# The triangular inverse of a gated delta rule: block transposes moved to VectorE, two last levels as small tiles

## Chip, cores and metric

The kernel runs on one core of one Trainium2 chip. The metric is the device time of one execution in microseconds. An execution covers the whole network below, with all weights read from HBM.

## What is computed

Two layers of a hybrid decoder on 256 positions of width 1024, all in float32. Each layer is a half-step SwiGLU FFN (width 2816), a mixer, and a second FFN. The mixer reads one normalised input through one projection whose columns feed three groups of heads: dilated-window attention (4 heads of 64), multi-scale pooling (256 channels), and a gated delta rule (4 heads of 128, chunks of 64 in the reference). The change is in the delta rule's inverse of a lower triangular matrix:

```python
def chunk_gated_delta_rule(q, k, v, g, beta):
    ...
    A = jnp.where(strict, jnp.einsum('nbhid,nbhjd->nbhij', kb, kc) * decay, 0.0)
    eye = jnp.eye(C, dtype=jnp.float32)
    T = lax.linalg.triangular_solve(eye + A, jnp.broadcast_to(eye, A.shape),
                                    left_side=True, lower=True)
    u = T @ vb
    w = T @ (kb * jnp.exp(g)[..., None])
    ...
```

```python
proj = h @ w_in[l]
aq, ak, av, pu, dq, dk, dv, dz, db, da = jnp.split(proj, split_at, axis=-1)
```

## The kernel before, in words

The program is written out by hand for each engine: TensorE, VectorE, ScalarE, GpSimd (POOL) and the DMA queue of SyncE (SP) each run their own list in order, and counting semaphores (`signal`, with `.at(layer, n)`) order them against each other.

**Weights.** Every weight piece of 128 x 1024 (512 KB) lands in one of six slots of `raw`. ScalarE rounds it to a high part `Wh` (`hi`, L1219), VectorE subtracts that to get a low part `Wl` (`lo`, L1647), and a product is then three matmuls, high by high, high by low and low by high (`three`, L660 to L662). The mixer has 33 pieces per layer. `MIX_SLOTS` says which slot each takes; `mix_free` (L1197) says which product must be over before a slot is cast again; `hi_mix(layer, i)` and `lo_mix(layer, i)` are the casts of piece i at the places where they stand in the two lists. The order of the pieces is: eight for attention and pooling, one with the gates, eight for query and key of the delta rule, four for its value, four for its gate z, eight of the output projection.

**Start of the mixer.** `enter_mixer` (L774) runs eight attention half tiles (`att_part`, L760: two pieces for one half of the positions, 24 matmuls of 128x256) and then the gates. `copy_half` (L1422, its copy in L1430) takes each out of PSUM. Parts 6 and 7 are the pooling channels; they are read only behind the inverse. Then come the query/key pieces with a convolution each (first tap on ScalarE, three taps on VectorE, L1834), the value pieces, gates, normalisation, decays, and the products of keys (L946) from which VectorE makes the matrices `LT` and `aT`.

**The inverse.** Here a chunk has 128 positions, so there are eight units (four heads, two halves c of the positions) of 128 x 128. `DT` and `Dm` hold the inverse found so far, one the transpose of the other. It starts from 2x2 blocks (`DT`, L1951), and each level n of `LEVELS = (2, 4, 8, 16, 32, 64)` doubles the block:

- `level_p` (L991): LT by Dm into banks 4 and 5; VectorE masks it into `PM` (L1959);
- `turn_d` (L998, all levels but the first): TensorE transposes `Dm` into banks 6 and 7, and ScalarE copies the new blocks into `DT` (L1527);
- `level_d` (L1015): DT by the even block columns of PM; ScalarE copies the result into `Dm` (L1538), in the last level into `DT` (L1017, L1540).

`Dm` itself comes from eight transposes on TensorE (L959), copied by ScalarE (L1507). V and K are transposed for later use (L966, L970). The casts of pieces 28, 29 and 30 stand behind the first three levels. POOL applies the rotary positions (L624 to L631); their result is transposed within the last level (`turn_qk`, L979). The first product with the finished inverse is L1101. Then follow the state, the scores (L1040, L1042), the pooling (L1132, L1134, L1156), the attention values (L1066 to L1068), and the eight output pieces (`out_product`).

```python
                for n in range(len(LEVELS)):
                    for c in range(HALVES):
                        level_p(n, c)
                    if n:
                        for c in range(HALVES):
                            turn_d(n - 1, c)
                    if n == len(LEVELS) - 1:
                        turn_qk()
                    for c in range(HALVES):
                        level_d(n, c)
```

Of the kernel before, what the change touches and what calls it, by code (L numbers as in the profile page):

```python
# [21 lines left out]
ALU = mybir.AluOpType  # L22
# [82 lines left out]
LEVELS = (2, 4, 8, 16, 32, 64)  # L105
# [10 lines left out]
C_ATT = C_LEVEL + P * len(LEVELS)  # L116
# [10 lines left out]
def constants():  # L127
# [7 lines left out]
    for n, s in enumerate(LEVELS):  # L135
        below = ((r // s) % 2 == 1) & (k // s == r // s - 1)
        c[:, C_LEVEL + n * P:C_LEVEL + (n + 1) * P] = np.where(r == k, 1.0, np.where(below, -1.0, 0.0))
# [30 lines left out]
def build(nc, x, positions, ffn1_norm, ffn1_w_gate, ffn1_w_up, ffn1_w_down, mix_norm, w_in, pool_w,  # L168
# [3 lines left out]
    with ctx:  # L172
# [190 lines left out]
        d0_turned = signal("d0_turned", 2)  # L363
        d_done = signal("d_done", 2 * len(LEVELS))
        p_done = signal("p_done", 2 * len(LEVELS))
        pm_done = signal("pm_done", 2 * len(LEVELS))
        dd_done = signal("dd_done", 2 * len(LEVELS))
        d_turned = signal("d_turned", 2 * len(LEVELS) - 2)
        dt_done = signal("dt_done", 2 * len(LEVELS))
        v_turned = signal("v_turned", 2)  # L370
# [65 lines left out]
        def _(sp):  # L436
# [16 lines left out]
            def load_ffn(layer, f):  # L453
                if f == 1:

                    gate, up, down = FFN[f]
                    for t in range(2):
                        srcs = (cols(gate, layer, t * P), cols(up, layer, t * P), down[layer, t * P:(t + 1) * P, :])
                        for j in range(3):
                            s = 3 * t + j  # L460
                            last = max(i for i in range(MIX_PIECES) if MIX_SLOTS[i] == s)
                            sp.wait_ge(*lo_cast.at(layer, MIX_BASE + last + 1))
                            sp.dma_start(raw[:, s, :] if j == 2 else piece(raw, s), srcs[j]).then_inc(landed[s].sem, 16)
                else:
                    load_tile(layer, f, 0, 0)
                    load_tile(layer, f, 1, 1)
# [6 lines left out]
            for layer in range(DEPTH):  # L473
# [3 lines left out]
                for i in range(MIX_PIECES):  # L477
# [3 lines left out]
                    if i < FIRST_OUT:  # L481
# [3 lines left out]
                                 else COL_DZ + (i - POS_Z) * P)  # L485
# [154 lines left out]
        def _(pe):  # L640
# [119 lines left out]
            def att_part(layer, j, ks, ready=None):  # L760

                g, c = divmod(j, 2)
                s0, s1, t = MIX_SLOTS[2 * g], MIX_SLOTS[2 * g + 1], slice(c * P, (c + 1) * P)
                pair = slice(s0, s1 + 1, s1 - s0)
                b = bank[ATT_BANKS[j]][:, 0:2 * P].rearrange("p (s c) -> p s c", s=2)
                for i in ks:
# [3 lines left out]
                    m = three(b, X0h[:, k, t], X0l[:, k, t], Wh[:, pair, k * P:(k + 1) * P],  # L770
# [3 lines left out]
            def enter_mixer(layer):  # L774
# [17 lines left out]
                for j in range(2, 8):  # L792
                    split(j // 2 * 2 + 1)
                    if j > 2:
                        pe.wait_ge(*att_read.at(layer, (1, 2, 3, 4, 6)[j - 3]))
# [69 lines left out]
            def mixer(layer):  # L865
# [7 lines left out]
                for i in range(8):  # L873
                    split(POS_QK + i)
                    if i == 0:
                        pe.wait_ge(*att_read.at(layer, 8))
# [78 lines left out]
                for c in range(HALVES):  # L955
                    pe.wait_ge(*dt0_done.at(layer, c + 1))
                    pe.wait_ge(*z_act.at(layer, c + 1))
                    for h in range(DN_HEADS):
                        m = nc.tensor.transpose(bank[4 + c][:, h * P:(h + 1) * P], DT[:, 4 * c + h, :], ident)  # L959
                    m.then_inc(d0_turned.sem, 1)  # L960

                for c in range(HALVES):
# [19 lines left out]

                def level_p(n, c):


                    pe.wait_ge(*d_done.at(layer, 2 * n + c + 1))
                    if n == 0:
                        pe.wait_ge(*lt_done.at(layer, c + 1))
                    for h in range(DN_HEADS):
# [5 lines left out]
                def turn_d(n, c):  # L995

                    for h in range(DN_HEADS):
                        m = nc.tensor.transpose(bank[6 + c][:, h * P:(h + 1) * P], Dm[:, 4 * c + h, :], ident)  # L998
                    m.then_inc(d_turned.sem, 1)

                def level_d(n, c):

                    s = LEVELS[n]
# [3 lines left out]
                    else:  # L1007
                        pe.wait_ge(*dt_done.at(layer, 2 * n + c - 1))
                    for h in range(DN_HEADS):
                        u = 4 * c + h  # L1010
                        out = bank[6 + c][:, h * 64:(h + 1) * 64].rearrange("p (n s) -> p n s", s=s)
                        pm = PM[:, u, :].rearrange("p (n a s) -> p n a s", a=2, s=s)
                        dt = DT[:, u, :].rearrange("p (n a s) -> p n a s", a=2, s=s)
                        if n < len(LEVELS) - 1:
                            m = nc.tensor.matmul(out, DT[:, u, :], pm[:, :, 0, :], start=True, stop=True)  # L1015
                        else:
                            m = nc.tensor.matmul(out, PM[:, u, :], dt[:, :, 1, :], start=True, stop=True)  # L1017
                    m.then_inc(dd_done.sem, 1)


                for n in range(len(LEVELS)):
                    for c in range(HALVES):
                        level_p(n, c)
                    if n:
                        for c in range(HALVES):
                            turn_d(n - 1, c)
# [1111 lines left out]
```

## Time and profile before

| what | value |
|---|---|
| median of 3 runs | 1093.78 us (1093.41 to 1094.16) |
| the profiled execution's own time | 1093.62 us |
| its span in the profile | 1091.8 us |
| TensorE (PE) busy | 1060.0 us, 97% of the span |
| VectorE (DVE) busy | 736.9 us, 67% |
| ScalarE (ACT) busy | 616.0 us, 56% |
| GpSimd (POOL) busy | 231.7 us, 21% |
| granted TensorE clock, mean | 0.997 of full speed |
| HBM | 163 GB/s over the span |

The profile is of one execution; its own time is 0.16 us under the median, and 1.8 us of it lie outside the span. Engines are named PE, DVE, ACT, POOL in its rows; PEld is TensorE's loading of weights, which overlaps its matmuls. A matmul of float32 operands shows as two starts in the rows of the trace; a transpose, or a matmul of rounded high and low operands (fp32r), shows as one. Durations of single matmuls overlap, so that the distance from start to start is what one costs. Layer 0's mixer starts near 197 us and ends near 357, layer 1's lies 537.5 us behind it.

### The profile page before, as it was taken

Reading aid. Unit: us, or ns where it says so; the run is one execution under the profiler, and the core shown is the slowest. Engines: PE = TensorE matmul, PEld = TensorE weight load, DVE = VectorE, ACT = ScalarE, POOL = GpSimd, SP = SyncE. Lnnn points to the kernel's source line nnn. Section 1 sums busy time; section 2 is a strip of 40 time slices with the busy share of each in tenths; the row PEclk is TensorE's granted clock in tenths of the full one; section 3 lists DMA queues with packets and bytes.
Section 4 is the critical chain, followed back from the end, with each engine's and each line's share of the span. In section 5 each row is a group of like instructions: output and inputs, shape, how many; then the busy total and the mean of one; then the engine's idle time right before and its main releaser. Section 6 shows DMA issues by size and latency. Waiting matters only on the chain.

```text
span 1091.8 us, 18536 instructions
## 1 busy us (share of the span) xinstructions
PE 1060.0 (97%) x6251; PEld 922.2 (84%) x6251; DVE 736.9 (67%) x1153; ACT 616.0 (56%) x1077; POOL 231.7 (21%) x257
## 2 busy tenths in 40 slices
PE   7999999899999999999999999999999999999997
PEld 6888888798987788888878888888988878888885
DVE  5666666878745766666676666668785657666665
ACT  6555555847644655555665555566665546555554
POOL 2212111295300121121122121112003003211212
PEclk9999999999999999999999999999999999999998
DMA  9766666562312476666646666666532035766660
GB/s 296 238 194 190 191 183 181 139 194 78 135 40 72 141 216 188 192 191 190 183 133 208 194 191 190 183 185 167 162 115 79 2 116 163 207 189 193 190 193 38
DMA packets 251895, 178.23 MB, mean 163 GB/s; under 512 B 5875, under 2 KB 237576, under 8 KB 251720
## 3 DMA queue, kind: packets, MB, share of 16 engines
q1 hardware_dynamic: 250880, 175.66, 54.3%
q0 software_dynamic: 336, 1.71, 0.4%
q8 instruction: 30, 0.49, 0.2%
q10 hardware_dynamic: 632, 0.23, 0.1%
q14 instruction: 17, 0.14, 0.0%
HBM read 176.53 MB, written 1.05 MB: 163 GB/s over the span
## 4 chain that ended last, share of the span: by engine, by line
PE 83%; DVE 10%; ACT 5%; issue 1%; DMA 0%; ACTq 0%; DVEq 0%
PE bank L678 28%; PE bank L681 15%; PE bank L660 11%; PE bank L661 10%; PE bank L662 10%; DVE Wl L1647 4%; PE bank L1015 2%; ACT Wh L1219 1%; DVE X L1692 1%; PE bank L991 1%; DVE xr L1823 1%; PE bank L723 1%; ACT X L1277 1%; DVE VT L1834 1%; DVE early L1865 1%
## 5 line engine op out<-in xcount | busy, mean ns | idle before, releaser
L1647 DVE TENSOR_TENSOR Wl<-raw,Wh 128x1024 fp32r<-128x1024 f32 x330 | 424.6, 1296 | 102.3 <-ACT Wh L1219 102.2
L1219 ACT ACTIVATE Wh<-raw 128x1024 fp32r<-128x1024 f32 x330 | 337.1, 1053 | 78.2 <-PE bank L662 75.6
L678 PE MATMUL bank<-X,Wh 128*128 128x512 f32 x1344 | 334.7, 391 | 0.0
L678 PEld LDWEIGHTS bank<-X,Wh 128*128 128x128 f32 x1344 | 246.7, 188 | 47.6
L577 POOL TENSOR_TENSOR gact<-gact,pooled 128x256 f32<-128x256 f32 x88 | 79.2, 900 | 626.4 <-DVE gact L1743 462.2
L681 PEld LDWEIGHTS bank<-X,Wl 128*128 128x128 f32 x1344 | 183.0, 190 | 14.0 <-DVE Wl L1647 1.2
L681 PE MATMUL bank<-X,Wl 128*128 128x256 f32 x1344 | 187.8, 283 | 0.0
L660 PE MATMUL bank<-Wh,aH 128*128 128x512 f32 x352 | 139.0, 395 | 2.0 <-DVE aL L1764 1.6
L661 PE MATMUL bank<-Wl,aH 128*128 128x512 f32 x352 | 138.0, 392 | 0.0
L662 PE MATMUL bank<-Wh,aL 128*128 128x512 f32 x352 | 137.1, 389 | 0.0
L1316 ACT ACTIVATE dec<-bank 128x256 f32<-128x256 f32 x88 | 33.6, 382 | 123.2 <-PE bank L681 122.2
L1333 ACT ACTIVATE aH<-hid 128x256 fp32r<-128x256 f32 x88 | 36.8, 418 | 92.4 <-DVE hid L1758 92.2
L579 POOL TENSOR_TENSOR gact<-gact,pooled 128x256 f32<-128x256 f32 x88 | 66.9, 760 | 79.9 <-ACT gact L1321 79.9
L660 PE MATMUL bank<-X,Wh 128*128 128x256 f32 x272 | 79.8, 293 | 0.0
L660 PEld LDWEIGHTS bank<-Wh,aH 128*128 128x128 f32 x352 | 66.4, 189 | 15.6 <-issue 4.2
L662 PEld LDWEIGHTS bank<-Wh,aL 128*128 128x128 f32 x352 | 66.1, 188 | 14.5
L1743 DVE TENSOR_TENSOR gact<-bank,dec 128x256 f32<-128x256 f32 x88 | 37.3, 424 | 58.9 <-ACT dec L1316 58.5
L662 PE MATMUL bank<-X,Wl 128*128 128x256 f32 x272 | 76.9, 283 | 0.0
L661 PE MATMUL bank<-X,Wh 128*128 128x256 f32 x272 | 76.8, 283 | 0.0
L661 PEld LDWEIGHTS bank<-Wl,aH 128*128 128x128 f32 x352 | 66.4, 189 | 10.4
L1751 DVE TENSOR_TENSOR hid<-bank,dec 128x256 f32<-128x256 f32 x88 | 37.3, 424 | 49.3 <-ACT dec L1327 49.3
L660 PE MATMUL bank<-Wh,X 128*128 128x256 f32 (+1 forms) x192 | 63.2, 329 | 4.8 <-DVE Wl L1647 3.0
(244 smaller groups left out, 1302.0 us busy)
## 6 DMA issues: line engine op xcount, KB each, us to landing
raw<-in_ffn_w_gate SPq DMA_DIRECT2D x88, 512.0 KB, 4.0
raw<-in_ffn_w_up SPq DMA_DIRECT2D x88, 512.0 KB, 3.7
raw<-in_ffn_w_down SPq DMA_DIRECT2D x88, 512.0 KB, 4.4
raw<-in_w_in SPq DMA_DIRECT2D x50, 512.0 KB, 3.9
raw<-in_w_out SPq DMA_DIRECT2D x16, 512.0 KB, 4.0
cst<-in_consts POOLq DMA_DIRECT2D x1, 1536.0 KB, 7.0
xr<-in_x SPq DMA_DIRECT2D x2, 512.0 KB, 4.4
norm_w<-in_final_norm SPq DMA_DIRECT2D x1, 512.0 KB, 5.7
```

What stands on the lines that cost most here:

```text
L577: nc.gpsimd.tensor_tensor(gact[:, par, :], gact[:, par, :], rB, ALU.mult).then_inc(gate_scaled.sem, 1)
L579: nc.gpsimd.tensor_tensor(gact[:, par, :], gact[:, par, :], rB, ALU.mult).then_inc(silu_scaled.sem, 1)
L660: nc.tensor.matmul(outp, lh, rh, start=start, stop=False)
L661: nc.tensor.matmul(outp, lh, rl, start=False, stop=False)
L662: return nc.tensor.matmul(outp, ll, rh, start=False, stop=stop)
L678: nc.tensor.matmul(b[:, :], piece(Wh, s)[:, k, :], X[:, k, :, :], start=k == 0, stop=False)
L681: m = nc.tensor.matmul(b[:, SEQ:], piece(Wl, s)[:, k, :], Xh[:, k, :], start=False, stop=k == KT - 1)
L1219: return nc.scalar.activation(Wh[:, s, :], raw[:, s, :], ACT.Copy).then_inc(hi_cast.sem, 1)
L1333: nc.scalar.activation(aH[:, par, :], hid[:, par, :], ACT.Copy).then_inc(ah_done.sem, 1)
L1647: return nc.vector.tensor_tensor(Wl[:, s, :], raw[:, s, :], Wh[:, s, :].bitcast(F32), ALU.subtract).then_inc(lo_cast.sem, 1)
L1743: nc.vector.tensor_tensor(gact[:, par, :], gbank[par][:, 0:SEQ], low[:, 0, par, :], ALU.add).then_inc(gsum_done.sem, 1)
L1751: nc.vector.tensor_tensor(hid[:, par, :], ubank[par][:, 0:SEQ], low[:, 1, par, :], ALU.add).then_inc(usum_done.sem, 1)
```

## The change

Six things change together.

1. *Attention half tiles.* Parts 6 and 7 (the pooling channels) leave `enter_mixer`. `att_late` runs them within the inverse, from the normalised input `Xh`, `Xl` instead of `X0h`, `X0l`, into banks 2 and 3, so that their copy needs no scale. Their two weight pieces move from positions 6 and 7 to 23 and 24 (`POS_LATE`), all pieces between come two positions earlier, and `MIX_SLOTS`, `mix_free` and the order in which the second FFN's first weights are loaded (slots 3, 4, 0, 1, 5, 2 instead of 0 to 5) follow.
2. *Transposes.* `turn_d` and the eight first transposes on TensorE go, and ScalarE's copies of their results with them. VectorE transposes all 32x32 blocks of four units in one instruction, `Dm` from `DT` once and `DT` from `Dm` once a level (`turn_blocks`). That is enough while no block is larger than 32.
3. *Even block columns.* `level_p` computes, and VectorE masks, only the 64 of 128 columns that `level_d` reads. The masks in the constants are half as wide. There are four levels left, 2 to 16.
4. *The level 32* works on blocks of 32x32 (`quarter_p`, `quarter_d`): 16 and 24 matmuls of 32 rows and 32 columns. The mask is a multiplication by -1 on 32 columns, and ScalarE copies three 32-row blocks for each half, two of them straight into `DT`.
5. *The level 64* works on blocks of 64x64 (`half_p`, `half_d`): 8 matmuls each, into the upper right block of `DT`.
6. *Casts.* Piece 28 keeps its place behind the first level. Pieces 29 and 30 are cast on ScalarE behind the inverse, on VectorE behind the output norms, `out_norm(1)`.

```diff
-POS_GATES, POS_QK, POS_V, POS_Z, FIRST_OUT = 8, 9, 17, 21, 25
-ATT_BANKS = (0, 1, 2, 0, 1, 2, 0, 2)
-MIX_SLOTS = [0, 1, 3, 4, 2, 5] * 4 + [0, 2, 5, 1, 3, 4, 0, 2, 5]
+POS_GATES, POS_QK, POS_V, POS_Z, POS_LATE, FIRST_OUT = 6, 7, 15, 19, 23, 25
+ATT_EARLY = 6
+ATT_BANKS = (0, 1, 2, 0, 1, 2, 2, 3)
+MIX_SLOTS = [0, 1, 3, 4, 2, 5] * 3 + [0, 1, 3, 4, 2, 0, 1] + [5, 3, 4, 2, 0, 1, 5, 2]
...
-LEVELS = (2, 4, 8, 16, 32, 64)
+LEVELS = (2, 4, 8, 16)
+N_LEVELS = len(LEVELS) + 2
+EVEN = P // 2
...
+                def att_late(j):
+
+                    split(POS_LATE + 1)
+                    pe.wait_ge(*z_act.at(layer, j - ATT_EARLY + 3))
+                    att_part(layer, j, range(KT)).then_inc(att_in.sem, 1)
...
-                    for h in range(DN_HEADS):
-                        u = 4 * c + h
-                        m = nc.tensor.matmul(bank[4 + c][:, h * P:(h + 1) * P], LT[:, u, :], Dm[:, u, :],
-                                             start=True, stop=True)
+                        pe.wait_ge(*d0_done.at(layer, c + 1))
+                        pe.wait_ge(*z_act.at(layer, c + 1))
+                    else:
+                        pe.wait_ge(*d_done.at(layer, 2 * (n - 1) + c + 1))
+                    for h, u in units(c):
+                        even = Dm[:, u, :].rearrange("p (n a s) -> p n a s", a=2, s=LEVELS[n])[:, :, 0, :]
+                        m = nc.tensor.matmul(bank[4 + c][:, h * EVEN:(h + 1) * EVEN], LT[:, u, :], even, start=True, stop=True)
...
+                def quarter_p(c):
+
+                    pe.wait_ge(*d_done.at(layer, 6 + c + 1))
+                    for h, u in units(c):
+                        for i in range(2):
+                            even, odd = slice(64 * i, 64 * i + 32), slice(64 * i + 32, 64 * i + 64)
+                            m = nc.tensor.matmul(bank[4 + c][odd, h * 32:(h + 1) * 32], LT[even, u, odd], Dm[even, u, even],
+                                                 start=True, stop=True)
+                    m.then_inc(p_done.sem, 1)
+
+                def quarter_d(c):
+
+
+                    pe.wait_ge(*pm_done.at(layer, 8 + c + 1))
+                    pe.wait_ge(*dt_done.at(layer, 6 + c + 1))
+                    q = [slice(32 * i, 32 * i + 32) for i in range(4)]
+                    for h, u in units(c):
+                        at = slice(h * 32, (h + 1) * 32)
+                        nc.tensor.matmul(bank[6 + c][q[1], at], DT[q[1], u, q[1]], PM[q[1], u, 0:32], start=True, stop=True)
+                        nc.tensor.matmul(bank[6 + c][q[0], at], PM[q[1], u, 0:32], DT[q[1], u, q[1]], start=True, stop=True)
+                        m = nc.tensor.matmul(bank[6 + c][q[2], at], PM[q[3], u, 0:32], DT[q[3], u, q[3]],
+                                             start=True, stop=True)
+                    m.then_inc(dd_done.sem, 1)
...
                 for n in range(len(LEVELS)):
                     for c in range(HALVES):
                         level_p(n, c)
-                    if n:
-                        for c in range(HALVES):
-                            turn_d(n - 1, c)
-                    if n == len(LEVELS) - 1:
-                        turn_qk()
                     for c in range(HALVES):
                         level_d(n, c)
+                for c in range(HALVES):
+                    quarter_p(c)
+                att_late(6)
+                for c in range(HALVES):
+                    quarter_d(c)
+                turn_qk()
+                for c in range(HALVES):
+                    half_p(c)
+                att_late(7)
+                for c in range(HALVES):
+                    half_d(c)
...
+                    dve.wait_ge(*dt0_done.at(layer, c + 1))
+                    nc.vector.transpose(Dm[:, u, :].rearrange("p u d -> p (u d)"),
+                                        DT[:, u, :].rearrange("p u d -> p (u d)")).then_inc(d0_done.sem, 1)
                 for i in (25, 26, 27):
                     lo_mix(layer, i)
```

**The order of the instructions, TensorE, from the transposes of V (VT) and K (QK) to the end of the second level.** In the rows `four` is the arena that holds LT, Dm and DT, and `x8` is eight in a row. Before:

```order
L959 MATMUL bank<-cst,four 128x128 x8
L966 MATMUL bank<-cst,VT 128x128 x8
L970 MATMUL bank<-cst,QK 128x128 x4
L991 MATMUL bank<-four 128x128 x8
L1015 MATMUL bank<-PM,four 128x64 x8
L991 MATMUL bank<-four 128x128 x8
L998 MATMUL bank<-cst,four 128x128 x8
L1015 MATMUL bank<-PM,four 128x64 x8
```

Now:

```order
L965 MATMUL bank<-cst,VT 128x128 x8
L969 MATMUL bank<-cst,QK 128x128 x4
L1001 MATMUL bank<-four 128x64 x8
L1012 MATMUL bank<-PM,four 128x64 x8
L1001 MATMUL bank<-four 128x64 x8
L1012 MATMUL bank<-PM,four 128x64 x8
```

The transposes with the identity (`cst`) are gone, and the first product of a level has 64 columns instead of 128.

**VectorE, from the matrix of 2x2 blocks (four<-four,cst) to the second of the levels.** Before:

```order
L1951 TENSOR_TENSOR four<-four,cst 128x512 x2
L1647 TENSOR_TENSOR Wl<-raw,Wh 128x1024 x3
L1959 TENSOR_TENSOR PM<-bank,cst 128x512 x2
L1647 TENSOR_TENSOR Wl<-raw,Wh 128x1024
L1959 TENSOR_TENSOR PM<-bank,cst 128x512 x2
L1647 TENSOR_TENSOR Wl<-raw,Wh 128x1024
```

Now:

```order
L1999 TENSOR_TENSOR four<-four,cst 128x512
L2001 STREAM_TRANSPOSE four<-four 128x512
L1999 TENSOR_TENSOR four<-four,cst 128x512
L2001 STREAM_TRANSPOSE four<-four 128x512
L1694 TENSOR_TENSOR Wl<-raw,Wh 128x1024 x3
L2018 TENSOR_TENSOR PM<-bank,cst 128x4x64 x2
L1694 TENSOR_TENSOR Wl<-raw,Wh 128x1024
L2009 STREAM_TRANSPOSE four<-four 128x512
L2018 TENSOR_TENSOR PM<-bank,cst 128x4x64
L2009 STREAM_TRANSPOSE four<-four 128x512
L2018 TENSOR_TENSOR PM<-bank,cst 128x4x64
```

The two first transposes stand ahead of three casts, and those of the second level stand behind the cast of piece 28 and ahead of the mask of their half.

**ScalarE, from the last level of the loop to the copy of the state (early<-bank).** Before:

```order
L1538 ACTIVATE four<-bank 128x8x32 x2
L1527 ACTIVATE four<-bank 128x8x32 x2
L1532 ACTIVATE qT<-bank 128x512
L1532 ACTIVATE kT<-bank 128x512
L1540 ACTIVATE four<-bank 128x4x64 x2
L1572 ACTIVATE early<-bank 128x512
```

Now:

```order
L1567 ACTIVATE four<-bank 128x16x16 x2
L1477 ACTIVATE big<-bank 128x256
L1575 ACTIVATE four<-bank 32x4x32
L1576 ACTIVATE four<-bank 32x4x32
L1577 ACTIVATE four<-bank 32x4x32
...
L1580 ACTIVATE kT<-bank 128x512
L1477 ACTIVATE big<-bank 128x256
L1585 ACTIVATE four<-bank 64x4x64 x2
L1263 ACTIVATE Wh<-raw 128x1024 x2
L1619 ACTIVATE early<-bank 128x512
```

The copies of the two late half tiles (`big`), the small blocks, and the casts of pieces 29 and 30 (`Wh`) now stand there.

## Rows read from the trace of the kernel before

**Rows 1.** The page: the chain that ended last, by engine.
```profile
PE 83%; DVE 10%; ACT 5%; issue 1%; DMA 0%; ACTq 0%; DVEq 0%
```

**Rows 2.** Stage table: from:to, length, busy us (instructions) by engine, clock, DMA, GB/s.
```profile
226.20:283.90 57.70, 57.70 (x441) 54.40 (x440) 48.28 (x99) 37.26 (x63) 33.35 (x33) 1.00 0.44 134
283.90:316.40 32.50, 30.35 (x263) 29.11 (x262) 14.64 (x18) 16.63 (x35) 9.62 (x8) 1.00 0.21 66
821.40:853.90 32.50, 30.42 (x264) 29.18 (x262) 14.61 (x18) 16.68 (x35) 9.57 (x8) 1.00 0.20 66
```

**Rows 3.** Groups, TensorE, 214.7 to 226.2 us: busy, mean ns | idle before.
```profile
L660 PE MATMUL bank<-Wh,X 128*128 128x256 f32 x32 | 9.1, 284 | 0.8 <-DVE Wl L1647 0.8
```

**Rows 4.** VectorE: timeline (start, length) at the gates; groups 232.5 to 255.5.
```profile
229.18 0.42 DVE L1871 TENSOR_TENSOR gact<-bank,pooled 128x256 f32<-128x256 f32 x1 [4.66 <-PE bank L662]
...
L1834 DVE SCALAR_TENSOR_TENSOR QK<-bank,prm,QK 128x255 f32<-128x255 f32 (+2 forms) x24 | 11.5, 480 | 2.6 <-ACT QK L1394 2.0
L1647 DVE TENSOR_TENSOR Wl<-raw,Wh 128x1024 fp32r<-128x1024 f32 x8 | 11.0, 1374 | 0.6 <-ACT Wh L1219 0.6
```

**Rows 5.** Timeline, ScalarE, the instruction behind the casts of pieces 23 and 24.
```profile
275.25 0.21 ACT L1490 ACTIVATE ga<-ga 128x8 f32<-128x8 f32 x1 [4.85 <-DVE ga L1919]
```

**Rows 6.** Timeline, start of the inverse and its first level.
```profile
283.55 3.49 DVE L1647 TENSOR_TENSOR Wl<-raw,Wh 128x1024 fp32r<-128x1024 f32 x3
286.62 2.05 PE L991 MATMUL bank<-four 128*128 128x128 f32 x16 [0.23 <-ACT four L1507]
287.81 0.69 DVE L1959 TENSOR_TENSOR PM<-bank,cst 128x512 f32<-128x512 f32 x1 [0.78 <-PE bank L991]
289.70 0.41 ACT L1538 ACTIVATE four<-bank 128x256 f32<-128x256 f32 x1 [1.18 <-PE bank L1015]
```

**Rows 7.** Groups, VectorE, 318 to 345 us: 128x512 within SBUF.
```profile
L2010 DVE TENSOR_TENSOR grow<-grow,ost 128x512 f32<-128x512 f32 x2 | 1.4, 692 | 0.1
```

**Rows 8.** Timeline, TensorE, second level and start of the third.
```profile
290.40 2.00 PE L991 MATMUL bank<-four 128*128 128x128 f32 x16
292.24 1.04 PE L998 MATMUL bank<-cst,four 128*128 128x128 f32 x8
293.93 2.00 PE L1015 MATMUL bank<-PM,four 128*128 128x64 f32 x16 [0.66 <-DVE PM L1959]
295.77 2.00 PE L991 MATMUL bank<-four 128*128 128x128 f32 x16
```

**Rows 9.** Timeline, last levels, value product, and the state's copy.
```profile
306.32 2.00 PE L991 MATMUL bank<-four 128*128 128x128 f32 x16
...
316.45 1.11 PE L1101 MATMUL bank<-early,four 128*128 128x128 f32 x8
...
320.33 0.60 ACT L1572 ACTIVATE early<-bank 128x512 f32<-128x512 f32 x1 [3.30 <-PE bank L1109]
```

**Rows 10.** Timeline, TensorE: 8 and 256 moving columns, and tiles of 64*64.
```profile
270.03 0.29 PE L922 MATMUL bank<-ga,cst 128*128 128x8 f32 x2
270.17 0.68 PE L928 MATMUL bank<-grow,cst 128*128 128x512 f32 x1
...
274.84 3.61 PE L946 MATMUL bank<-QK 128*128 128x256 f32 x16
...
327.84 1.08 PE L1156 MATMUL bank<-pooled,pwl 64*64 64x256 f32 x8
```

**Rows 11.** Timeline, TensorE, from full matmuls to tiles of 128*64.
```profile
337.29 0.39 PE L662 MATMUL bank<-Wh,X 128*128 128x512 f32 x1
337.61 0.43 PE L1066 MATMUL bank<-prT,big 128*64 128x128 f32 x2
```

**Rows 12.** Timeline, behind the inverse: VectorE and TensorE.
```profile
336.48 0.42 DVE L2048 TENSOR_TENSOR X<-bank,X 128x256 fp32r<-128x256 f32 x1
338.71 0.48 PE L660 MATMUL bank<-Wh,X 128*128 128x512 f32 x1
356.81 1.09 PE L687 MATMUL bank<-cst,xr 128*128 128x128 f32 x8 [0.73 <-DVE xr L1823]
```

More of the change, by code:

```diff
@@ L136, in constants @@
         below = ((r // s) % 2 == 1) & (k // s == r // s - 1)
-        c[:, C_LEVEL + n * P:C_LEVEL + (n + 1) * P] = np.where(r == k, 1.0, np.where(below, -1.0, 0.0))
+        full = np.where(r == k, 1.0, np.where(below, -1.0, 0.0))
+        c[:, C_LEVEL + n * EVEN:C_LEVEL + (n + 1) * EVEN] = full.reshape(P, -1, 2, s)[:, :, 0, :].reshape(P, EVEN)
     c[:, C_ONES:C_ONES + P] = 1.0
@@ L456, in load_ffn @@
                     gate, up, down = FFN[f]
[L457 to L463, printed above, removed]
+                    for s in (3, 4, 0, 1, 5, 2):
+                        t, j = divmod(s, 3)
+                        last = max(i for i in range(MIX_PIECES) if MIX_SLOTS[i] == s)
+                        sp.wait_ge(*lo_cast.at(layer, MIX_BASE + last + 1))
+                        src = (cols(gate, layer, t * P), cols(up, layer, t * P), down[layer, t * P:(t + 1) * P, :])[j]
+                        sp.dma_start(raw[:, s, :] if j == 2 else piece(raw, s), src).then_inc(landed[s].sem, 16)
                 else:
@@ L791, in enter_mixer @@
                 row_root(layer, 1)
[L792 removed]
+                for j in range(2, ATT_EARLY):
                     split(j // 2 * 2 + 1)
                     if j > 2:
[L795 removed]
+                        pe.wait_ge(*att_read.at(layer, j - 2))
                     att_part(layer, j, range(KT)).then_inc(att_in.sem, 1)
@@ L1007, in level_d @@
                     else:
[L1008 to L1017, printed above, removed]
+                        pe.wait_ge(*dt_done.at(layer, 2 * (n - 1) + c + 1))
@@ L1505, in mixer @@
                 for c in range(HALVES):
-                    act.wait_ge(*d0_turned.at(layer, c + 1))
-                    nc.scalar.activation(Dm[:, 4 * c:4 * c + 4, :].rearrange("p u d -> p (u d)"), bank[4 + c][:, :],
-                                         ACT.Copy).then_inc(d_done.sem, 1)
-                for c in range(HALVES):
                     act.wait_ge(*v_turned.at(layer, c + 1))
@@ L1961, in mixer @@
                                                 ALU.mult).then_inc(pm_done.sem, 1)
-                    if n < 3:
-                        lo_mix(layer, FIRST_OUT + 3 + n)
+                    if n == 0:
+                        lo_mix(layer, 28)
+                for c in range(HALVES):
+                    turn_blocks(len(LEVELS), c)
+                    dve.wait_ge(*p_done.at(layer, 8 + c + 1))
+                    nc.vector.tensor_scalar(PM[:, 4 * c:4 * c + 4, 0:32],
+                                            bank[4 + c][:, 0:P].rearrange("p (u t) -> p u t", u=4), -1.0, None,
+                                            ALU.mult).then_inc(pm_done.sem, 1)
@@ L1965, in new_values @@
+                for c in range(HALVES):
+                    dve.wait_ge(*p_done.at(layer, 10 + c + 1))
+                    nc.vector.tensor_scalar(PM[EVEN:, 4 * c:4 * c + 4, 0:EVEN],
+                                            bank[4 + c][EVEN:, 0:256].rearrange("p (u t) -> p u t", u=4), -1.0, None,
+                                            ALU.mult).then_inc(pm_done.sem, 1)
                 def new_values(c):
```

137 lines of the change are left out of this document (82 added, 55 removed).

## The prediction

> **What bounds the kernel now.** Read the page first, then a table by stage, then single rows. The page gives TensorE 83% of the chain that ended last [rows 1]. The stage table cuts layer 0's mixer, at full granted clock: from 226 to 284 us TensorE is busy without a gap, and only in the inverse (283.9 to 316.4) does it miss 2.15 of 32.5 us; layer 1's inverse reads the same [rows 2]. So in the mixer the order of TensorE's own work sets the time, and one microsecond of it removed is a microsecond only if VectorE and ScalarE can follow. The 0.2% that counts as a change below is 2.2 us, about what a measurement of this kernel can tell from none.
>
> All times below are layer 0's; layer 1 repeats them, so the sum is doubled.
>
> **Part 1: two attention half tiles leave the start of the mixer.** A half tile is 24 products of 128x256. The last four of them end at 226.2 us with 96 starts in 11.5 us, 0.120 each, and none waits but the first [rows 3]. Two half tiles are 48 x 0.120 = 5.76 us. Do the others follow? VectorE is idle 4.66 us before the gate copy at 229.18 [rows 4], so its casts are ahead. In the convolutions it has 1.37 (cast) + 1.44 (three taps of 0.48) = 2.81 us for each piece against TensorE's 24 x 0.120 = 2.88 [rows 3, 4]: close, but under it. What follows from 258 us, the gate arithmetic, normalisation and decays, hangs on the first value pieces of TensorE, and so moves with it. Two ScalarE casts get later occupants of their slots to wait for: piece 23 the last value piece, piece 24 the first z piece. Both are the products TensorE runs next to them, so that the two waits together are at most one piece, 2.88 us, and ScalarE is idle 4.85 us right behind them [rows 5]: nothing. Without that cover they would cost up to 2.9 us. **-5.76.** From here I keep the old clock times and subtract 5.76 at the end.
>
> **Part 2: start of the inverse.** TensorE loses 8 transposes (0.93 us), ScalarE two copies of 0.54. Before, the first product waited for those copies, which stood behind z and a table load, until 286.62 [rows 6]. Now the block transposes run on VectorE, ahead of three casts that end at 287.04 [rows 6], so the casts end 2T later, T one transpose of 128x512. The trace has no such transpose. From below it isn't cheaper than a row of half its size, 0.42 for 128x256 [rows 4]; from above, twice the 0.69 us that a 128x512 row takes, 1.38 [rows 7]. I take 0.69, the row of its own size. Then casts end at 288.4, the first mask (now 256 columns, 0.42 [rows 4]) at 288.9, and the first level's second products start at 288.95, where they started at the first mask's end, 288.5 [rows 6]. The next level begins at 290.85 instead of 290.40: **+0.45.** The product itself now starts at once, without use: VectorE is behind.
>
> **Part 3: levels.** A product costs two starts of 0.115 us, 128 columns or 64: 16 starts last 290.40 to 292.24 and 293.93 to 295.77 [rows 8]. Halving the columns of the first product therefore saves TensorE nothing; what goes is the 8 transposes (0.93) and the wait for the mask (0.66). The level behind cast 28 takes 5.37 now. After: VectorE ends that cast at 293.6 instead of 293.3, then transpose, mask, transpose, mask (0.69 + 0.4 each with issue) before the second half: its second products start at 294.7 and 295.75, the level ends at 296.7 against 295.77: **+0.93 in total so far**. The two levels behind it are free of casts (29 and 30 are moved), and need max(TensorE 4 x 0.93 = 3.7; VectorE 2 x (0.69 + 0.40) = 2.2). The chain of a half, 1.19 to the mask, 0.4, 1.14 to the copy, 0.4, 0.2 [rows 6], is 3.4. So 3.73 each against 5.27 (295.77 to 306.32 for two [rows 8, 9]): 296.7 + 7.45 = 304.15 against 306.3 before, **-3.1**.
>
> **Part 4: levels 32 and 64 as tiles.** Before, 306.32 to 316.45, 10.13 us [rows 9]. After there are 16 + 24 + 8 + 8 = 56 small products, 112 starts. No row has a tile of 32x32 or 64x64 with so few columns. Above: 0.115, as a full one. Below: 0.115 x 32/128 = 0.03, if the weights alone count. Nearest: two starts with 8 columns take 0.14, 0.07 each; tiles of 64x64 with 256 moving columns make eight starts in 1.08 us, the last one's own duration in it, about 0.10 each, where 16 full ones take 3.61, about 0.21 each [rows 10], so tiles do overlap. I take 0.06: 112 x 0.06 = 6.7. Added: two half tiles 5.76, the query/key transposes 0.93, six switches between full array and tiles at 0.1 (a start that comes 0.32 after a 512-column one instead of 0.23 [rows 11]) = 0.6, and about 0.4 until the last copy lets the value product go. Sum 14.4: it starts near 318.5 instead of 316.45. **+2.05 in all against before.** The other engines hide: ScalarE's six small copies and casts 29, 30 (2.0 us) fit into its 3.30 us gap before the state copy [rows 9].
>
> On a switch the row says 0.1. The Trainium skill (TensorEngine Tiling, Key Properties) says that changing the tiling mode drains the engine. If a drain cost the whole 0.39 us that such a product lasts, six would add 1.7 us a layer and the time would be 1089.9 us; the row is what I go by.
>
> **Part 5: behind the inverse.** Casts 29 and 30 on VectorE (2.36) now stand ahead of the low part of attention at 336.48, which so ends at 339.3; TensorE wants it at 338.71: +0.6. In return the first cast of the FFN's weights waits for the fifth output piece instead of the sixth, so VectorE is done with its part of these casts when the residual update can start, and TensorE's 0.73 us wait for it at 356.81 shrinks by about 0.6 [rows 12]. The loads: slots 3 and 4 early; slots 0 and 1 wait for the moved casts, to about 338, some 10 us ahead of their use. **0.**
>
> **Sum.** Per layer -5.76 + 2.05 = -3.7, two layers -7.4: 1093.62 (profiled execution) - 7.4 = 1086.2; the median of the runs is 0.16 higher, so **1086.4 us**.
>
> **Rivals.** (a) *Tiles cost as much as full products* (0.115 from the first small product on; it decides from 0.093, where 112 x 0.033 eats the 3.7). 112 x 0.055 = 6.2 more a layer: 1086.4 + 12.3 = 1098.7, slower. For it: halving columns to 64 saved nothing. Against: the overlap in rows 10. Chance 0.07.
> (b) *VectorE becomes the bound of the levels*, T = 1.38: the start loses 1.4 us, the levels take 4.4 instead of 3.73 and the cast level 1.4 more: about 4.2 a layer, 1094.8, no change. For it: VectorE stands last at the first mask. Against: 128x512 rows at 0.69. 0.09.
> (c) *The 5.76 us don't get through*, because VectorE's run from 258 us on is the bound: then only +2.05 a layer stays, 1097.9, slower. For it: from 261.5 to 287 it hardly pauses. Against: it starts on TensorE's products. 0.06.
> (d) *Row groups serialise at a bank*: the 32x32 products alternate row groups and write one bank; if each waited for the other's whole 0.275 us (16 starts 0.115 apart last 2.00 [rows 8]), 80 starts x 0.215 = 17 us a layer, 1121. The 64x64 products of L1156 write one bank from two row groups too, and start about 0.10 apart [rows 10], which speaks against it. 0.03. That different row tiles can't use one bank at the same time is a rule of the Trainium skill (TensorEngine Tiling, Gotcha 1: PSUM Pressure).
> (e) The forecast's mechanism, with its own bounds: tiles at 0.03 save 6.7 more (1079.7), T = 0.42 about two. 0.75.
>
> **How the numbers follow.** Likeliest is (e). Faster: (e) without a slight share that ends within 2.2 us, 0.74. Same: (b) and that share, 0.10. Slower: (a), (c), (d), 0.16. The range goes from 1080, tiles at their lower price, to 1097 and so takes in (b) and half of a mixture of (a) and (c); left out are (d), the rest of those two and the extreme low end, under 0.2.
>
> **What would show it.** Right: first query piece on TensorE 5.7 us earlier in the mixer; STREAM_TRANSPOSE near 0.69; levels 8 and 16 at 3.7 to 3.9 us; small products starting every 0.05 to 0.07; the value product about 3.7 us earlier. Wrong: small products at 0.1 or more; transposes over 1 us with TensorE waiting for VectorE in each level; a granted clock below full in the inverse; a TensorE wait of over 1 us for attention's low part or for FFN weights.

## The result, and the profile after

The changed kernel takes **1105.56 us** (median of 4 executions, 1103.55 to 1106.79), the kernel before 1093.61 beside it: ratio 1.0106, interval 1.0093 to 1.0119. The forecast was 1086.4, range 1080 to 1097. It is slower by 11.9 us, and the forecast missed by 19.2.

From the page of the kernel after (busy time by engine, then TensorE's granted clock in 40 slices):

```profile
span 1103.6 us, 18478 instructions
PE 1069.2 (97%) x6251; PEld 930.9 (84%) x6251; DVE 746.6 (68%) x1173; ACT 609.1 (55%) x1061; POOL 232.3 (21%) x257
PEclk9999999999679999999999999999995999999999
```

The clock line has a dip near each layer's inverse. The stage table of layer 0, cut at the first product, the first small tile and the value product (columns as in [rows 2]):

```profile
226.20:279.80 53.60, 53.60 (x408) 50.31 (x407) 47.41 (x99) 37.62 (x64) 34.11 (x37) 1.00 0.48 146
279.80:309.50 29.70, 26.21 (x130) 25.80 (x128) 13.60 (x19) 5.80 (x12) 9.76 (x8) 0.57 0.23 71
309.50:322.40 12.90, 12.90 (x169) 12.12 (x168) 1.94 (x5) 4.21 (x12) 0.00 (x0) 0.80 0.01 1
```

In the four levels the mean clock is 0.57 of 2.4 GHz, so they mostly run at the lower level, 1.2 GHz. Before, the whole inverse had 1.00 [rows 2]. The timeline of TensorE shows where it begins:

```profile
278.49 1.03 PE L965 MATMUL bank<-cst,VT 128*128 128x128 f32 x8
279.80 1.90 PE L1001 MATMUL bank<-four 128*128 128x64 f32 x16
284.98 3.67 PE L1012 MATMUL bank<-PM,four 128*128 128x64 f32 x16 [3.28 <-DVE PM L2018]
288.44 3.62 PE L1001 MATMUL bank<-four 128*128 128x64 f32 x16
...
309.53 1.18 PE L1022 MATMUL bank<-four 32*32 32x32 f32 x32
...
317.15 1.14 PE L1044 MATMUL bank<-four 64*64 64x64 f32 x16
...
322.43 1.16 PE L1143 MATMUL bank<-early,four 128*128 128x128 f32 x8
```

The first product runs at full clock (1.90 for 16 starts). TensorE then stands still for 3.28 us, waiting for the first mask. Sixteen starts take 3.62 us from then on, where they took 2.00 before [rows 8], and the value product comes at 322.43, before at 316.45 [rows 9]. The table in slices of 2 us dates the fall and the return:

```profile
282.00:284.00 2.00, 0.00 (x0) 0.00 (x0) 2.00 (x2) 0.00 (x0) 1.85 (x2) 1.00 0.40 160
284.00:286.00 2.00, 1.02 (x5) 1.03 (x6) 1.25 (x3) 0.00 (x0) 2.00 (x3) 0.50 0.00 0
...
312.00:314.00 2.00, 2.00 (x11) 2.00 (x10) 0.00 (x0) 0.00 (x0) 0.00 (x0) 0.50 0.00 0
314.00:316.00 2.00, 2.00 (x57) 1.87 (x57) 0.00 (x0) 0.38 (x1) 0.00 (x0) 0.82 0.00 0
```

The clock falls at about 284.0, while TensorE stands still, and returns at 314.7, late in the attention half tile (310.63 to 315.5): 30 us at 0.50, though TensorE is busy in nearly all of them. Layer 1 has a stop of 3.67 us and the same picture (low from 826.7 to 857.5).

Why the mask is late is on VectorE and GpSimd:

```profile
278.35 0.71 DVE L2001 STREAM_TRANSPOSE four<-four 128x512 f32<-128x512 f32 x1
278.98 5.60 DVE L1694 TENSOR_TENSOR Wl<-raw,Wh 128x1024 fp32r<-128x1024 f32 x3
284.51 0.74 DVE L2018 TENSOR_TENSOR PM<-bank,cst 128x256 f32<-128x256 f32 x2
```
```profile
279.61 1.69 POOL L627 TENSOR_TENSOR qkr<-big,trig 128x512 f32<-128x512 f32 x1 [3.16 <-PE bank L965]
281.27 2.24 POOL L628 TENSOR_TENSOR VT<-big,trig 128x512 f32<-128x512 f32 x1
```

The three casts ahead of the mask take 5.60 us where they took 3.49 [rows 6]. GpSimd's rotary work starts on the transposed V (L965). Before, it began 2.5 us behind the first cast (283.55 [rows 6]):

```profile
286.04 2.13 POOL L624 TENSOR_TENSOR qkr<-big,trig 128x512 f32<-128x512 f32 x1 [3.56 <-PE bank L966]
```

Now it begins 0.6 us behind it, for two reasons: TensorE transposes V right behind the projections, without the eight transposes that stood there, and VectorE's two block transposes put the casts later. So the rotary work falls onto the casts.

### The profile page after: what moved, and what is told of

It is laid out like the page before. It is cut to its first block, busy times and chain, and to the rows that moved or that the text cites. A ratio compares the mean times of both kernels' runs of the same rounds, so it can differ in the third digit from the quotient of the medians.

```text
span 1103.6 us, 18478 instructions
## 1 busy us (share of the span) xinstructions
PE 1069.2 (97%) x6251; PEld 930.9 (84%) x6251; DVE 746.6 (68%) x1173; ACT 609.1 (55%) x1061; POOL 232.3 (21%) x257
## 4 chain that ended last, share of the span: by engine, by line
PE 83%; DVE 12%; ACT 3%; issue 1%; DMA 1%; ACTq 0%; DVEq 0%
PE bank L681 28%; PE bank L684 15%; PE bank L663 11%; PE bank L664 10%; PE bank L665 10%; DVE Wl L1694 4%; PE bank L1012 3%; PE bank L1001 1%; DVE X L1739 1%; DVE xr L1870 1%; PE bank L726 1%; ACT X L1321 1%; DVE VT L1881 1%; DVE early L1912 1%; DMA hid<-in_ffn_norm 1%
```

## Experiments

Each run is an edit of the kernel after, or of the one before where the text says so; all ran beside the kernel before (medians 1093.62 to 1093.82 us). Waits and times of single rows are layer 0's where no layer is named.

**Run 1, rotary work later.** GpSimd waits for the first masks before it starts.

```diff
                 pool.wait_ge(*v_turned.at(layer, 2))
+                pool.wait_ge(*pm_done.at(layer, 2))
```

> The changed kernel, with GpSimd's rotary work held back until the first two masks are written, so that it no longer runs beside VectorE's three weight casts. Theory 1 (the clock): the casts fall from 5.6 to about 3.5 us, TensorE's wait before the first level's second products from 3.3 and 3.7 us to 1.2 to 1.6, the granted clock stays at 1.00 through the inverse, and the time is 1082 to 1088 us. Theory 2 (the work of the new levels itself, with its halved columns and small tiles, lets the clock fall): the wait shrinks as above but the clock still falls to 0.50 in the inverse, and only the 2 x 2.1 us of the wait come back: about 1101.

Measured: 1099.38 us (ratio 1.0052, 1.0025 to 1.0080). TensorE and VectorE (columns as above):

```profile
279.13 3.45 DVE L1695 TENSOR_TENSOR Wl<-raw,Wh 128x1024 fp32r<-128x1024 f32 x3
```
```profile
282.97 2.47 PE L1013 MATMUL bank<-PM,four 128*128 128x64 f32 x16 [1.15 <-DVE PM L2019]
285.24 3.62 PE L1002 MATMUL bank<-four 128*128 128x64 f32 x16
```

With GpSimd's work away the three casts take 3.45 us: the 2.15 us more were its doing. The Trainium skill (SBUF — State Buffer, SBUF: two separate sides) has the rule that a VectorE instruction with two SBUF inputs and a GpSimd one that reads SBUF exclude each other; the trace agrees, 5.60 us beside it and 3.45 without. But a stop of 1.15 us is left (1.53 in layer 1), and the clock falls all the same: 3.62 us for 16 starts from 285.24 on, at 0.50 until 311.6 us.

**Run 2, a half tile in the first gap.** `att_late(6)` and `copy_half(6)` move from behind `quarter_p` to between the first `level_p` and `level_d`.

> The changed kernel, with the first late attention half tile run between the first and the second products of the first level, where TensorE waits, instead of behind the level 32's first products; its copy on ScalarE moves with it. Theory 1: TensorE's wait falls to about 0.5 us, the clock stays at 1.00, and the time is 1078 to 1083 us: about 22 us under the changed kernel, most of it from levels that go at full clock. Theory 2: the clock still falls once the levels run; the gain is the filled wait alone, 2 x 2.9 us, about 1100.

Measured: 1098.87 us (1.0046, 1.0024 to 1.0069). The first wait is 0.42 us (0.80 in layer 1) and the clock holds. In the second level TensorE waits 1.83 us: cast 28, for which VectorE sits idle 3.13 us until ScalarE has cast the same piece, stands ahead of that level's transposes and masks. There the clock falls (0.71 in 290 to 292 us, then 0.50 up to 318).

**Run 3, work without use in the first gap**: 24 products of a half tile more, the rest as it was.

> The changed kernel, with 24 useless products (the first late half tile computed once more, into the same bank) put into the same wait of TensorE; nothing else moves and nothing is saved. Theory 1: the idle time becomes work, the clock stays at 1.00, and the kernel gets faster by adding work: 1083 to 1088 us. Theory 2: the clock falls anyway and the time stays near 1105. Theory 3 (the time went to the wait for the casts itself, not to what it does to the clock): no change either, since the masks come no earlier.

Measured: 1102.44 us (1.0079). First wait 0.39 us, second 1.82 us at 291 us, and the clock falls there as in run 2. With 5.8 us of added work it is still 3 us under the kernel after.

**Run 4, a stop in the kernel before**: six VectorE multiplications without use ahead of the first masks.

> The kernel before, with six idle multiplications of 128x512 put on VectorE ahead of the first level's masks (4.2 us), so that TensorE waits about 3.4 us there. Theory 1: the clock falls to 0.50 as in the changed kernel and stays there through most of the inverse, whose products then take twice their time: 2 x (3.4 + 12 to 20), 1120 to 1140 us. Theories 2 and 3: the clock holds and the time is 1093.6 + 2 x 3.4 = about 1101.

Measured: 1116.30 us (1.0205). TensorE stops 8.08 us, where 3.4 were expected, so that this stop is more than twice the one to be copied. The clock falls:

```profile
297.53 3.68 PE L1016 MATMUL bank<-PM,four 128*128 128x64 f32 x16 [8.08 <-DVE PM L1965]
301.00 3.14 PE L992 MATMUL bank<-four 128*128 128x128 f32 x16
303.98 1.04 PE L999 MATMUL bank<-cst,four 128*128 128x128 f32 x8
```

The kernel before loses the clock too if it must stop this long, but has it back at 303.4 us, within its next level: 5.9 us after TensorE resumed (7.4 in layer 1), against 30 us in the kernel after. That left two suspects, the stop and what the levels do after it. The next four runs, with the kernel after and run 2, cross the two.

**Run 5, casts spread.** No cast ahead of the first masks; one behind the masks of each of the four levels.

```diff
-                for i in (25, 26, 27):
-                    lo_mix(layer, i)
...
-                    if n == 0:
-                        lo_mix(layer, 28)
+                    lo_mix(layer, 25 + n)
```

> The kernel after, with the three weight casts (pieces 25 to 27) that stand ahead of the first masks moved: one behind the masks of each of the first four products (25 to 28), so that no mask waits for three casts beside GpSimd's rotary work. The products still have 64 columns. Theory 'wait' (the long stop of TensorE before the first mask, 3.3 and 3.7 us, takes the clock, and nothing else does): the first wait is under 0.7 us, the granted clock stays at 1.00 in the inverse, levels of 16 starts take 1.9 us, and the time is about 1105.6 - 2 x 9.5 = 1087. Theory 'work' (with the transposes gone and 64 columns the levels hold too little work for the full clock, with or without a long stop): the first wait is as short, yet the clock falls to 0.50 within the first two levels and stays there until the half tile, as in the run with the half tile moved: 1097 to 1101.

**Run 6, full columns.** `level_p` computes all 128 columns and the mask reads the even ones; the stop stays.

```diff
-                        even = Dm[:, u, :].rearrange("p (n a s) -> p n a s", a=2, s=LEVELS[n])[:, :, 0, :]
-                        m = nc.tensor.matmul(bank[4 + c][:, h * EVEN:(h + 1) * EVEN], LT[:, u, :], even, start=True, stop=True)
+                        m = nc.tensor.matmul(bank[4 + c][:, h * P:(h + 1) * P], LT[:, u, :], Dm[:, u, :], start=True, stop=True)
```

> The kernel after, with the first product of each level on all 128 columns (the mask reads the even ones), the casts where the change put them, so the stop of 3.3 us stays. Starts are 0.115 apart with 64 or 128 columns at full clock, so by counts nothing changes. Theory 'work': the clock still falls after the stop but comes back within some 10 us, as it did in the kernel before with a stop of 7.5 us put in (there in 10): low for 8 to 12 us instead of 31, levels 2 to 16 partly at 1.9, 1105.6 - 2 x 6 = about 1093. Theory 'wait' (only the stop matters and the clock comes back only with attention's 256-column products): low until about 315 us as in the kernel after, 1104 to 1107, or later still, since at half clock 128 columns take twice as long to stream as 64.

**Run 7, runs 2 and 6 together.**

> The kernel with the last half tile put into the gap of the first level (e2: 1098.9, first wait 0.42, next 1.83, clock lost at about 291 us), now with the first product of each level on all 128 columns. Theory 'work': what is left of waits (under 2 us) does not take the clock from levels with 128 columns, or gives it back soon: about 1082 to 1088. Theory 'wait': the 1.83 us wait takes it as before: 1097 to 1101.

**Run 8, runs 5 and 6 together.**

> Both repairs at once: casts 25 to 28 one behind the masks of each level, and 128 columns in the first product. If either theory is right the clock stays at 1.00 or nearly. The levels each carry a cast (1.2 to 1.9 us) on VectorE beside two transposes and two masks (2.2), so they take up to 4.1 us where 3.73 was forecast: about 1084 to 1090. If the clock still falls to 0.50 and stays, both theories are wrong and it is the lost transposes on TensorE: 1098 or more.

Measured:

| | 64 columns | 128 columns |
|---|---|---|
| stop of 3.3 us | 1105.56 (after) | 1086.78 (run 6; 1083.9 to 1089.1) |
| waits 0.4 and 1.8 us | 1098.87 (run 2) | 1079.04 (run 7; 1078.5 to 1084.3) |
| casts spread, no stop | **1070.66** (run 5) | 1070.97 (run 8) |

Both of the times expected for run 5 were too high (1087, and 1097 or more), and so were those for run 6 (1093, and 1104 or more) and run 8 (1084 or more); run 7's median lies under its 1082 to 1088.

Run 5 has ratio 0.9792 (0.9773 to 0.9811): the change with three casts moved is 23.0 us *faster* than the kernel before and 34.9 faster than the change as it was. Its timeline and stage table:

```profile
280.48 1.90 PE L1001 MATMUL bank<-four 128*128 128x64 f32 x16
282.21 1.95 PE L1012 MATMUL bank<-PM,four 128*128 128x64 f32 x16
...
294.81 0.98 PE L1022 MATMUL bank<-four 32*32 32x32 f32 x32
...
300.43 1.14 PE L1044 MATMUL bank<-four 64*64 64x64 f32 x16
...
304.57 1.14 PE L1053 MATMUL bank<-four,PM 64*64 64x64 f32 x16
305.71 1.16 PE L1143 MATMUL bank<-early,four 128*128 128x128 f32 x8
```
```profile
280.40:294.80 14.40, 14.40 (x131) 14.34 (x128) 11.56 (x19) 5.89 (x12) 9.57 (x8) 1.00 0.12 38
294.80:305.70 10.90, 10.80 (x169) 9.97 (x168) 2.44 (x6) 4.22 (x12) 0.00 (x0) 1.00 0.50 146
```

TensorE has no wait in the four levels, and the clock stays at 1.00. So 64 columns alone don't cost the clock: theory "work" falls for the case without a stop, and 128 columns gain nothing there. They matter once it is lost. TensorE in run 6, with the stop:

```profile
285.11 3.67 PE L1011 MATMUL bank<-PM,four 128*128 128x64 f32 x16 [3.23 <-DVE PM L2019]
288.57 3.05 PE L1000 MATMUL bank<-four 128*128 128x128 f32 x16
292.40 2.03 PE L1011 MATMUL bank<-PM,four 128*128 128x64 f32 x16 [0.77 <-DVE PM L2019]
```

Run 6 is back at full clock by 291 us, in its second level, where the kernel after needs until 315. Neither theory had it alone: the clock falls at the stop, and how long it stays low depends on the work behind it.

A stop doesn't always take it. Run 7 has almost the same second wait in both layers, 1.77 and 1.78 us. Layer 0:

```profile
290.89 2.58 PE L1011 MATMUL bank<-PM,four 128*128 128x64 f32 x16 [1.77 <-DVE PM L2021]
293.26 3.12 PE L1000 MATMUL bank<-four 128*128 128x128 f32 x16
```

and layer 1, where the clock stays at 1.00 throughout:

```profile
821.99 2.03 PE L1011 MATMUL bank<-PM,four 128*128 128x64 f32 x16 [1.78 <-DVE PM L2021]
823.86 2.00 PE L1000 MATMUL bank<-four 128*128 128x128 f32 x16
```

What decides between the two is not shown.

**Runs 10 and 11, a stop with another cause.** Three VectorE multiplications without use ahead of the first masks, in run 5's kernel and in run 8's.

> The fast version of run 5 (casts spread, 64 columns, no stop, 1070.7) with one stop put back that has nothing to do with casts or GpSimd: three multiplications of 128x512 on VectorE without use, ahead of the first masks. TensorE is to stop for 1.5 to 2.5 us once per layer. If a single stop takes the clock and 64-column levels don't bring it back, the clock reads 0.50 from that stop to the half tile, seven groups of 16 starts take 3.6 us instead of 1.9 (12 us a layer), and the time is 1096 to 1100. If the stop has to be longer, or it was the casts or GpSimd's work that did it, only the stop itself is added: 1074 to 1076.

> The same stop in the version with 128 columns in the first product (run 8, 1071.0). If those columns bring the clock back, it is low for 5 to 10 us instead of some 23, and the time is 1080 to 1086, at least 12 us under the run with 64 columns beside it. If the columns have no part in it, both runs give the same time within 3 us.

Measured: run 10 1098.01 us, run 11 1080.35 us. TensorE's waits are 1.92 and 1.87 us (2.20 and 2.14 in layer 1). Run 10:

```profile
283.79 3.08 PE L1013 MATMUL bank<-PM,four 128*128 128x64 f32 x16 [1.92 <-DVE PM L2022]
286.67 3.62 PE L1002 MATMUL bank<-four 128*128 128x64 f32 x16
```

and run 11:

```profile
283.96 2.35 PE L1012 MATMUL bank<-PM,four 128*128 128x64 f32 x16 [1.87 <-DVE PM L2023]
286.11 3.32 PE L1001 MATMUL bank<-four 128*128 128x128 f32 x16
289.26 1.90 PE L1012 MATMUL bank<-PM,four 128*128 128x64 f32 x16
```

One stop of about 2 us a layer, from work that has nothing to do with casts or GpSimd, costs 27 us (by the median) with 64 columns and 9 with 128; some 4 us of either are the stops themselves. Run 10's eight executions lie in two groups, three at 1087.3 to 1088.8 and five at 1097.5 to 1101.6, so that the cost is 17 us or 27 to 31. The profile shown is of the second kind, with the clock low for 27.3 us in layer 0 and 30.7 in layer 1. No profile of the first kind was taken, but each execution's mean clock is on record: 0.972 to 0.976 in the five, 0.983 to 0.986 in the three, 0.997 to 0.999 in run 5. As an estimate, 0.998 less 0.985, over 1087 us and at the lower level, is 28 us of low clock, one layer's share. So in these three the same stop most likely took the clock in one layer only.

**Run 12, half tiles ahead.** Run 5's kernel with `att_late(6)` and `att_late(7)` ahead of the first product, nothing between the tiled levels.

> The fast version of run 5 with both attention half tiles ahead of the first product of the inverse, none between the tiled levels. TensorE's work is the same. What they hid must show: between the small products and what follows each chain of mask, product and copy now stops TensorE, by 0.4 to 1.5 us at four places, 2 to 4 us a layer, and a clock that falls there falls into the tiled levels and the value products. Without a fall of the clock 1075 to 1079; with one 1085 to 1100. If the half tiles hid nothing, 1070.7 as before.

Measured: 1074.92 us, 4.3 more than run 5. In layer 0 only one wait appears, 0.35 us at the 32x32 products, and the value product comes 0.20 us later than in run 5. In layer 1 a wait of 0.34 us at 828.44, among small products, is followed by the lower clock:

```profile
826.00:828.00 2.00, 1.90 (x64) 1.71 (x63) 2.00 (x4) 0.77 (x2) 0.00 (x0) 1.00 0.23 29
828.00:830.00 2.00, 1.66 (x42) 1.52 (x32) 0.39 (x2) 1.72 (x7) 0.00 (x0) 0.81 0.89 298
830.00:832.00 2.00, 2.00 (x19) 1.67 (x18) 0.43 (x1) 1.05 (x2) 0.00 (x0) 0.50 1.03 313
```

Layer 0's wait of the same length at the same place took nothing, so the wait's length alone doesn't decide. The time lies just under the range expected without a fall (1075 to 1079), though the clock did fall. The half tiles hide little waiting. Of the 4.3 us most is the clock's, by an estimate: it is low for 10 us in layer 1.

**Run 9, half the columns in the kernel before**, levels 2 to 32, the rest as it was.

> The kernel before, with the first product of levels 2 to 32 on the 64 even columns alone (the masks as four small operations a half, which lengthens them by some 0.3 us); transposes on TensorE, casts and half tiles where they were. Its waits for the masks are 0.6 to 0.9 us. If 64 columns matter only after a stop of over 1 us, the clock stays at 1.00 and the time is 1093 to 1099 from longer masks. If 64 columns with such short waits already cost the clock, it reads 0.50 in the inverse and the time is 1105 to 1125. A gain from halving (under 1091) would speak against the reading that a start takes 0.115 us with either number of columns.

Measured: 1093.38 us (0.9999, 0.9987 to 1.0011), clock 1.00 in the inverse with waits of up to 0.76 us. One of its eight executions took 1097.82 us at a mean clock of 0.992, the others 0.998 or 0.999; it wasn't profiled, and where it lost the clock is open. Halving the columns alone gains nothing and costs nothing, as the start distance of 0.115 us said [rows 8].

**Run 13, casts spread in the kernel before**, pieces 25 to 30, one behind the masks of each level.

> The kernel before, with the same move of casts as in run 5: pieces 25 to 30 one behind the masks of each level, none ahead of the first. If the 23 us that run 5 gained over the kernel before come from the casts' place, this kernel gains too (under 1085). If they come from the change and the casts only kept it from showing, then nothing moves here, since in the kernel before the first mask waits for TensorE and the later ones for the chain of transposes: 1091 to 1095.

Measured: 1091.21 us (0.9975, 0.9964 to 0.9985), 2.6 us less. The 1.8 us of waits for masks in layer 0 vanish. There cast 28 waited for ScalarE and held up the masks; cast 25 in its place had its high part long before. Of run 5's 23.0 us some 2.6 are thus had by moving casts without the change; the rest needs the change.

## Why the prediction was wrong, by its own steps

**The step that failed** is the one that the whole sum stood on without a term of its own: levels, tiles and half tiles were all priced at 1.00 of the clock [rows 2], and a fall was named only as a sign of being wrong, with no rival and no price. I took TensorE's waits in the inverse as costing their own length. Before, those for a mask were 0.66 us [rows 8] and that was true. Runs 5, 8, 10 and 11 show that one stop of about 2 us a layer costs 27 us (median) with 64 columns and 9 with 128.

**Part 2, start of the inverse.** T = 0.69 was right (0.71). The casts were to end 2T later and last 3.49 us; the term that was mis-sized is their length, 5.60, because GpSimd's work moved onto them. Of the parts moved earlier I had followed TensorE, VectorE and ScalarE, but not GpSimd, which starts on V's transposes. The second products started at 284.98; the forecast, 288.95 - 5.76, was 283.19: 1.8 us a layer. The larger error is in its last words. "The product itself now starts at once, without use: VectorE is behind" describes a TensorE that stands still, for 1.5 us even by the forecast's own end (from 279.80 + 1.90 to 283.19), which is more than the stop at which the clock fell in run 1's layer 0. No price beyond its length was put on it.

**Part 3, levels.** Forecast 15.2 us from the first second products to the first small tile (288.95 to 304.15), measured 24.55 (284.98 to 309.53): 9.35 us a layer, the bulk of the miss. The lower clock accounts for all of it: at full clock and without the casts in front, run 5 takes 12.60 for the same stretch (282.21 to 294.81), a level of 32 starts 3.57 against the 3.73 forecast; the mechanism was right.

**Part 4, tiles.** The price of a small start, 0.06 us, was too high. In run 5 the 32 starts of `quarter_p` take 0.91 us (294.81 to 295.72), 0.028 each, and the 48 of `quarter_d` lie within 0.51 (298.78 to 299.29), 0.011 each. The two sets of 64x64 take 1.07 and 1.14, 0.07 each. All 112 with switches and the last copy come to 3.75 us, where the forecast had 6.7 + 0.6 + 0.4 = 7.7. Against it a half tile behind the level takes 3.06 instead of 2.88. In the kernel after this part is 12.90 instead of 14.4, in spite of the clock.

The check of the sum: 1.8 + 9.35 - 1.5 = 9.65 a layer, 19.3 for two, against a miss of 19.2. Layer 1 bears the doubling out: the value product comes 5.98 us later than before in layer 0 and 11.72 later in layer 1 (865.69 against 853.97), so that layer 1 adds 5.74.

**Part 1** was right: the first transposes behind the gate pieces (L903, 252.42; before L897, 257.97) come 5.55 us earlier, 5.76 forecast, and the first product starts at 279.80 instead of 286.62. **Part 5** was right too: TensorE waits 0.36 us for the low part of attention (0.6 forecast), and the 0.73 us wait for the residual update [rows 12] is gone.

**The rivals.** (a), tiles as dear as full products, (b), VectorE's transposes as the bound, and (c), the 5.76 not getting through, did not happen. (b) was also priced too high: its levels of 4.4 us stand on no row, and by part 3's own rule 2 x (1.38 + 0.40) = 3.56 would have stayed under 3.73. (d), row groups that serialise at a bank, would have cost 17 us a layer; the 48 starts of `quarter_d` write each bank from two row groups and are 0.011 us apart. The rule of the Trainium skill (TensorEngine Tiling, Gotcha 1: PSUM Pressure) that different row tiles can't use one bank at the same time doesn't show in these starts. None of the rivals was what happened; the missing one was "the first mask is later than the product, TensorE stops, and the clock goes".

With the clock held the forecast was off on the other side. Run 5 is 15.7 us below 1086.4: 3.6 us a layer from the levels (294.81 against 304.15 - 5.76 = 298.39) and 3.5 from the tiles (10.90 against 14.4), 14.2 for both layers; the other 1.5 lies outside these stretches and wasn't followed.

## What to carry to other kernels

- Before taking work away from a critical engine, ask where it will then stand still, and look at the granted clock for what that costs. A stop can cost far more than its length: 17 to 31 us for two of about 2 us in run 10. The work behind it (columns per product here) is then no longer free to shrink.
- If a step moves earlier, go through every engine that starts on it, also those with time to spare: the rotary work on GpSimd was off the path, and cost by what it ran beside.
- A slow change can be a fast one with one thing out of place. Three casts moved by a few lines turned +12 us into -23.

## What the runs showed of the hardware that was not expected

- The granted clock fell in or right after stops of TensorE of 1.15 and 1.53 us (run 1), 1.8 to 2.2 (runs 2, 3, 10, 11, layer 0 of run 7), 3.2 to 3.7 (after, run 6) and 8.1 (run 4), and once around a wait of 0.34 us among small tiles (run 12, layer 1). It held through 0.76 us (run 9), 0.80 (run 2, layer 1), 0.35 (run 12, layer 0) and also 1.78 (run 7, layer 1). No length of a stop in these traces separates the two.
- At the lower clock, products of 128x64 ran for 24 us with TensorE hardly idle, and the clock did not come back; with 128 columns in every second group of 16 it was low for 3.3 to 6.8 us and back 4.5 to 7.1 us after TensorE resumed (runs 6, 7, 11), in the kernel before 5.9 and 7.4 us after (run 4).
- At full clock the number of columns, 64 or 128, hardly matters to 16 starts of float32 (1.95 and 2.00 us in runs 5 and 8), and at the lower one neither: 3.62 (after) and 3.73 (run 11, layer 1).
- 32x32 products of float32 start down to 0.011 us apart (48 starts of `quarter_d` in 0.51 us, run 5).
- A block transpose of 128x512 in float32 on VectorE takes 0.70 us (run 5).
- Three 128x1024 subtractions within SBUF on VectorE take 3.45 us alone (run 1) and 5.60 (after) beside GpSimd's multiplications, which are stretched too: L628 takes 2.24 us there and 1.27 (287.03) where VectorE is idle.
